# Two norms that follow a finished expert sum: weights spread earlier, the next tile's vector and two turns reordered

## The chip, the cores and the metric

The kernel runs on one core of one Trainium2 chip. The metric is the device time of one execution in microseconds (us). Three executions before the change took 2376.06, 2380.5 and 2389.85 us, median 2380.5. All arithmetic is float32.

## The reference, cut to what matters

Two transformer-like blocks follow each other on 512 rows of 1024 elements. The first ends in a layer of single-neuron experts: each row picks 128 experts (8 heads, 16 each), takes the dot product of its normed vector with 128 rows of `expert_u`, and adds up 128 rows of `expert_v` with the resulting weights. Then it is normed, and the second block begins with a norm of its own.

```python
def one(xb):                      # 64 rows at a time
    ...                           # eidx (rows, 8, 16), gate g
    u = expert_u[eidx]
    v = expert_v[eidx]
    act = jax.nn.gelu(jnp.einsum('td,thkd->thk', xb, u), approximate=False)
    return jnp.einsum('thk,thkd->td', g * act, v)
...
h = h + ff                        # after the experts
out = rmsnorm(h, ln_final)        # end of the first block
# second block
h = rmsnorm_2(x, norm1_g)         # attention and pooling on h @ w_in
x = x + mixed @ w_out
h2 = rmsnorm_2(x, norm2_g)
x = x + (silu(h2 @ w_gate) * (h2 @ w_up)) @ w_down
return rmsnorm_2(x, final_g)
```

## The kernel before, in words

The 512 rows are four tiles of 128. The first block's mixer and expert choice run first, then the second block in the order of `SECOND` (line 38): attention of tiles 0 and 1, attention of tile 2, the feed-forward of tiles 0 to 2, attention of tile 3, its feed-forward, the output.

The experts run beside all this as a second stream. For each tile GpSimd (POOL, L1172) gathers 128 rows of `peer_u`, one indirect DMA of 128 x 4 KB each, into a ring of 16 slots; VectorE (DVE, L2745) takes one dot product per gathered row with the **dot vector**, which stands in two PSUM banks (`wide`, banks 6 and 7): TensorE spreads the norm weights into it (`urow`, L1471) and DVE multiplies it by the tile's row and its factor (L2734). Then 128 rows of `peer_v` are gathered and summed: for tiles 0 and 3 on DVE (L2769), for tiles 1 and 2 (`VPE`) on TensorE in 32 **row units** of four gathered rows each (`rows`, L1481), accumulated in the same banks 6 and 7.

When a tile's sum is complete, the unit `h3` follows. On DVE: the sum is added to the tile (L2776, "h2e"); the tile is multiplied by the norm weights in two halves (L2787, "gained") that TensorE has spread over two banks (`gain`, in the unit `h3` at L1496, eight matmuls); some small operations and a root make the factor (L2791 to L2811); two multiplications write the normed tile (L2815). On ScalarE (ACT): the squares of the tile (L2121), written to banks 6 and 7, the squares of the two halves (L1690), also to banks 6 and 7, and the root (L1678). Banks 6 and 7 are thereby taken by "squares" until ACT is done, and the next tile's `urow` waits for it.

The order of every engine's program is one list of units, made by `make_plan`. The main stream yields after each step; `QUOTA` says how many expert rows are due within each stage of it (in sixths, thirds and so on of the stage's cost), and `more()` appends that much of `plan_experts`. A yield of `("h3", t)` appends all that is left up to tile t's `h3`. Each engine works through its units strictly in the order of the list. PSUM banks are given out by small rings, `lo` (banks 0 to 2) and `hi` (3 to 5) at the places of this change.

Around the end of tile 1 the list reads: row units 28 to 31 between the last steps of choosing tile 3's experts, `h3 1`, one choosing step (L2486), `urow 2`, dots 0 to 3, `chosen`, dots 4 to 6, then `norm` and two `turn` units of the attention of tiles 0 and 1 (a turn transposes a tile on TensorE and scales it by a diagonal matrix that DVE makes at L2244; ACT copies it out at L1734).

Around the end of tile 2 it reads:

```
rows 2 28 | wout 0 1 0 0 | wout 0 1 0 1 | rows 2 29 | norm (fe,0) | turn (fe,0) 0 | rows 2 30
turn (fe,0) 1 | rows 2 31 | h3 2 | norm (at,2) | turn (at,2) 0 | urow 3 | dot 3 0 | dot 3 1
fgate 2 | dot 3 2 | qku 2 0 0 | dot 3 3 | qku 2 0 1 | dot 3 4 | fsoft 2 | dot 3 5 ...
```

`wout` is the attention's output product of tiles 0 and 1 (its result is added at L2667); `norm (fe,0)` and the two turns make the feed-forward's input from it, which is not used before the feed-forward; `turn (at,2)` is tile 2's own, and `fgate`, `qku` and `fsoft` (L2595 on DVE) begin its attention. `IDLE` puts 14 matmuls without use ahead of `turn (at,2)`.

## Time and profile before

| what | value |
|---|---|
| median of three runs | 2380.5 us |
| span of the profiled execution | 2541.9 us |
| its own time apart from the span | not recorded |
| TensorE (PE) busy | 2151.2 us, 85% |
| VectorE (DVE) busy | 1499.3 us, 59% |
| ScalarE (ACT) busy | 653.7 us, 26% |
| GpSimd (POOL) busy | 1020.5 us, 40% |
| moved by DMA | 839.81 MB, mean 330 GB/s |
| mean granted TensorE clock | 0.898 |

The span of the profiled execution is 161.4 us longer than the median of the timed runs, so each time read from the trace belongs to an execution that is slower than the timed ones. A row of the timeline is: start in us from the span's start, duration in us, engine, line, operation, what it writes and reads, count, and in brackets how long the engine was idle before it and what ended that. "remote" stands where no instruction of the trace was found that ended the wait, "issue" where the engine waited for nothing that the profile shows. A float32 matmul has two records.

### The profile page before, as it was taken

How to read it: one execution, taken by the hardware profiler on the slowest of the kernel's cores; microseconds unless marked ns; L12 is line 12 of the kernel's file. 1: busy time of each engine (PE TensorE's matmuls, PEld its weight loads, DVE VectorE, ACT ScalarE, POOL GpSimd, SP SyncE). 2: the span in 40 equal slices, each digit the busy share in tenths (PEclk: the TensorE clock that was granted, in tenths of full speed). 3: DMA queues.
4: the chain of work that ended last, by engine and by line, in shares of the span. 5: the costliest groups of instructions: out<-in, count | busy, mean ns of one | idle time of the engine just before them, and what ended most of it. 6: DMA issues, size and time to landing. Idle time of an engine off the chain costs nothing.

```text
span 2541.9 us, 29123 instructions
## 1 busy us (share of the span) xinstructions
PE 2151.2 (85%) x10694; PEld 1516.7 (60%) x10694; DVE 1499.3 (59%) x3505; ACT 653.7 (26%) x1838; POOL 1020.5 (40%) x1028
## 2 busy tenths in 40 slices
PE   8999998999999986996675366276879799999998
PEld 7999785666666975874431254221366555545695
DVE  3441179999999368647454677710067665886321
ACT  6772235566555121001010101110122000001220
POOL 0000014555665113435566554566544544772000
PEclk8999999999998997998886567578887899999999
DMA  6767568999999978999999888999978998998485
GB/s 237 245 231 240 215 254 298 404 397 393 390 377 337 378 274 320 398 356 380 363 394 361 308 335 320 366 343 364 409 307 323 411 348 313 412 412 355 157 316 173
DMA packets 196750, 839.81 MB, mean 330 GB/s; under 512 B 22000, under 2 KB 22384, under 8 KB 164864
## 3 DMA queue, kind: packets, MB, share of 16 engines
q0 software_dynamic: 147456, 536.94, 54.8%
q1 hardware_dynamic: 43808, 290.72, 30.6%
q10 hardware_dynamic: 5344, 10.29, 1.3%
q8 instruction: 85, 1.39, 0.2%
q14 instruction: 57, 0.47, 0.0%
HBM read 835.70 MB, written 2.16 MB: 330 GB/s over the span
## 4 chain that ended last, share of the span: by engine, by line
PE 60%; DVE 15%; issue 10%; ACT 6%; POOL 5%; another core or an unknown queue 3%; DMA 2%; ACTq 0%; DVEq 0%; SPq 0%
PE ps L1200 59%; DVE rows L2745 7%; POOL rows L1172 5%; DVE ps L2769 1%; DMA rows<-in_pv,eidxT 1%; DVE h L2769 1%; DVE arena L2297 1%; DMA wr<-in_wso 1%; ACT arena L1734 1%; ACT L1871 1%; ACT arena L1865 0%; DMA wr<-in_wgate 0%; ACT L1801 0%; DVE arena L2359 0%
## 5 line engine op out<-in xcount | busy, mean ns | idle before, releaser
L1172 POOL DMA_INDIRECT rows<-in_pu,eidx x512 | 485.3, 948 | 936.6 <-DVE dots L2745 368.7
L1200 PE MATMUL ps<-arena,wr 128*128 128x128 f32 (+4 forms) x3968 | 771.9, 354 | 26.0 <-DMA wr<-in_wso 9.2
L1200 PEld LDWEIGHTS ps<-arena,wr 128*128 128x128 f32 x3968 | 606.9, 195 | 168.6 <-issue 27.3
L2745 DVE CUSTOM_DVE_ANT_0 rows<-rows,ps 128x1024 f32<-128x1024 f32 x512 | 594.0, 1217 | 11.3 <-DMA rows<-in_pu,eidx 5.5
L1200 PE MATMUL ps<-hT,wr 128*128 128x128 f32 (+2 forms) x1600 | 369.7, 390 | 44.6 <-issue 41.3
L1172 POOL DMA_INDIRECT rows<-in_pv,eidx x256 | 289.2, 1130 | 207.0 <-DVE h L2769 101.4
L1200 PEld LDWEIGHTS ps<-hT,wr 128*128 128x128 f32 x1600 | 262.5, 199 | 148.7 <-issue 57.6
L1172 POOL DMA_INDIRECT rows<-in_pv,eidxT x256 | 245.7, 960 | 142.9 <-issue 68.6
L1200 PE MATMUL ps<-rows,wz 128*32 128x512 f32 x1024 | 180.7, 778 | 78.5 <-DMA rows<-in_pv,eidxT 57.1
L1200 PE MATMUL ps<-wr,arena 128*128 128x256 f32 (+2 forms) x704 | 180.7, 412 | 2.1 <-ACT arena L1943 2.1
L2769 DVE SCALAR_TENSOR_TENSOR h<-rows,wgt,h 128x1024 f32<-128x1024 f32 x132 | 169.0, 1280 | 5.7 <-DMA rows<-in_pv,eidx 4.8
L2769 DVE SCALAR_TENSOR_TENSOR ps<-rows,wgt,ps 128x1024 f32<-128x1024 f32 x122 | 156.6, 1284 | 8.1 <-DMA rows<-in_pv,eidx 8.1
L1200 PEld LDWEIGHTS ps<-wr,arena 128*128 128x128 f32 x704 | 129.5, 192 | 49.1 <-issue 33.7
L1200 PEld LDWEIGHTS ps<-rows,wz 128*32 128x32 f32 x1024 | 39.9, 129 | 198.1 <-issue 194.2
L1200 PE MATMUL ps<-wr,fT 128*128 128x512 f32 x304 | 135.2, 602 | 5.5 <-issue 5.5
L1200 PEld LDWEIGHTS ps<-wr,fT 128*128 128x128 f32 x304 | 58.5, 193 | 80.2 <-issue 80.2
L2297 DVE SCALAR_TENSOR_TENSOR arena<-arena,vec 128x144 f32<-128x144 f32 (+2 forms) x160 | 74.8, 468 | 51.9 <-ACT arena L1794 44.7
L2401 DVE TENSOR_TENSOR arena<-arena,ps 128x256 f32<-128x256 f32 (+1 forms) x24 | 12.3, 511 | 151.2 <-PE ps L1200 146.9
L2044 ACT ACTIVATE fT<-ps 128x384 f32<-128x384 f32 (+1 forms) x44 | 16.9, 385 | 276.9 <-PE ps L1200 145.5
L2681 DVE TENSOR_TENSOR fT<-fT,ps 128x384 f32<-128x384 f32 (+1 forms) x44 | 18.5, 421 | 112.7 <-PE ps L1200 86.3
L1200 PE MATMUL ps<-arena 128*128 128x64 f32 (+3 forms) x352 | 64.5, 314 | 11.8 <-DVE arena L2356 6.6
L2633 DVE CUSTOM_DVE_ANT_0 lg<-ps,cb 128x128 f32<-128x128 f32 (+3 forms) x32 | 15.7, 492 | 93.9 <-PE ps L1200 52.2
(403 smaller groups left out, 2258.3 us busy)
## 6 DMA issues: line engine op xcount, KB each, us to landing
wr<-in_wg SPq DMA_DIRECT2D x48, 1024.0 KB
wr<-in_wgu SPq DMA_DIRECT2D x33, 1024.0 KB
wr<-in_wgate SPq DMA_DIRECT2D x24, 1024.0 KB
wr<-in_wso SPq DMA_DIRECT2D x24, 1024.0 KB
wr<-in_wq SPq DMA_DIRECT2D x16, 1152.0 KB
wr<-in_wsc SPq DMA_DIRECT2D x16, 1024.0 KB
wr<-in_wqku SPq DMA_DIRECT2D x15, 1024.0 KB
wr<-in_wdn SPq DMA_DIRECT2D x14, 1024.0 KB
```

The source lines that it names most:

```text
L1172: e.indirect_dma_start(ring[slot_of[i]], None, A[table], bass.IndirectOffsetOnAxis(ap=index[:, t, k:k + 1], axis=0)).then_inc(gathered[slo ...
L1200: return e.matmul(o, l, r, start=start, stop=stop, skip_group_check=True)
L1734: e.activation(dst[:, kk, col:col + w_], b[:, 128 * k:128 * k + w_], ACT.Copy, scale=gv[:, kk:kk + 1]).then_inc(*act.up("turn", tag, s, half))
L1871: e.activation(m[f"mt{c % 2}"].rearrange("p a b -> p (a b)"), fall.rearrange("p a b -> p (a b)"), ACT.Exp, scale=-1.0).then_inc(*act.up("s ...
L2044: e.activation(FD[t0]["fT"][:, j, :], b[:, 0:nr], ACT.Silu).then_inc(*act.up("silu", t0, j))
L2297: e.scalar_tensor_tensor(out=tx[:, c1:n] if k < 3 else xg[:, s_, c1:n], in0=x[:, k + c1:k + n], scalar=W["convw"][:, q4 + k:q4 + k + 1], i ...
L2401: e.tensor_tensor(flat, flat, b[:, 0:2 * nr], MUL).then_inc(*dve.up("mg", q, j))
L2633: e.tensor_tensor_reduce(m[f"lg{p}"][:, 0:kn], b[:, 0:kn], cb[:, h, 0:kn], 1.0, NEG, ADD, ALU.max, mxx[:, p:p + 1]).then_inc(*dve.up("fron ...
L2681: e.tensor_tensor(fT[:, j, :], fT[:, j, :], b[:, 0:nr], MUL).then_inc(*dve.up("fT", t0, j))
L2745: e.tensor_tensor_reduce(row, row, wide[:], 1.0, 0.0, MUL, ADD, dots[:, k:k + 1]).then_inc(*dve.up(*u))
L2769: e.scalar_tensor_tensor(out=sum_, in0=row, scalar=wgt[:, k:k + 1], in1=sum_, op0=MUL, op1=ADD).then_inc(*dve.up(*u))
```

## The change

Five edits, all of order and place:

- `gain` becomes a unit of its own, and for tiles 1 and 2 (those before a tile in `URGENT`) it is put ahead of row unit 28, with its two banks from `hi`. For tiles 0 and 3 it stays behind the sum, in `lo`.
- `h3` is split into the units `h2e`, `gained` and `h3`. For tiles 1 and 2 the next tile's `urow` (TensorE's spread and DVE's multiplication) is put between `gained` and `h3`.
- For tiles 1 and 2 banks 6 and 7 are no longer taken for squares: ACT writes the squares to `junk` (tile 1) or to a tile of the attention that is done (`AT[0]["mx"]`, tile 2), both in SBUF.
- In the attention of tiles 0 and 1, `norm (fe,0)` stays where it was, then `("h3", 2)` is yielded, and the two turns `(fe,0)` come after it.
- The 14 idle matmuls ahead of `turn (at,2)` are taken away.

```diff
@@ -37,6 +37,7 @@
 GROUPS = ((0, 1), (1, 2), (2, 4))
 SECOND = (("attend", 0, 2), ("attend", 2, 3), ("feed", 0, 3), ("attend", 3, 4), ("feed", 3, 4), ("out", 3, 4))
 VPE = (1, 2)
+URGENT = (2, 3)
 VW = 1.5
 SX = 1.8
 PLACES = ("early", "ring", "ring")
@@ -46,7 +47,7 @@
 ARENA = 18144
 AHEAD_GATES = (4, 3, 2)
 GATE_BUFFERS = (4, 3, 2)
-IDLE = {("at", 2): 14, ("at", 3): 2}
+IDLE = {("at", 3): 2}
 AHEAD = 2
 PLAIN = (("at", 3), ("fd", 3),)
 SPARE = 6
@@ -618,7 +619,10 @@
                 wout(hf, part, t)
                 yield True
     if t0 == 0:
-        yield from plan_turn(pl, ("fe", t0), range(nt))
+        fe = plan_turn(pl, ("fe", t0), range(nt))
+        yield from until("normed", fe)
+        yield ("h3", t1)
+        yield from fe
 
 
 def plan_feed(pl, A, t0, t1, outs=()):
@@ -718,10 +722,19 @@
         for half in range(2):
             pl.hold((key, t, half), 6 + half, emptied)
 
+    def gain(t, ring):
+        for half in range(2):
+            pl.take(("gain", t, half), ring, ("dve", "gained" if ("at", t) in PLAIN else "h3", t, half))
+        pl.add("gain", t)
+
+    def urow(t):
+        both("urow", t, ("dve", "dot", t, 127))
+        pl.add("urow", t, v=vc(1024))
+
     for t in range(NT):
         yield ("chosen", t, 0)
-        both("urow", t, ("dve", "dot", t, 127))
-        pl.add("urow", t, v=vc(1024))
+        if t not in URGENT:
+            urow(t)
         for k in range(128):
             if k and k * pieces_of(t) % 128 == 0:
                 yield ("chosen", t, k * pieces_of(t) // 128)
@@ -736,6 +749,8 @@
             yield 1
         both("sums", t, ("dve", "h2e", t))
         for k in range(32):
+            if k == 28 and t + 1 in URGENT:
+                gain(t, "hi")
             if t in VPE:
                 pl.add("rows", t, k)
                 if k < 31:
@@ -745,9 +760,14 @@
                     pl.add("vrow", t, i, v=1.3)
                 if k < 31:
                     yield 4
-        both("squares", t, ("act", "squares", ("h3", t)))
-        for half in range(2):
-            pl.take(("gain", t, half), "lo", ("dve", "gained" if ("at", t) in PLAIN else "h3", t, half))
+        pl.add("h2e", t)
+        if t + 1 in URGENT:
+            pl.add("gained", t)
+            urow(t + 1)
+        else:
+            both("squares", t, ("act", "squares", ("h3", t)))
+            gain(t, "lo")
+            pl.add("gained", t)
         pl.add("h3", t, v=4 * vc(1024))
         yield 4
 
@@ -1493,7 +1513,7 @@
                                    ring[slot_of[i]][:, 512 * half:512 * half + 512], k == 0, k == 31)
                     x.then_inc(*pe.up(*u))
 
-                elif kind == "h3":
+                elif kind == "gain":
                     t = u[1]
                     for half in range(2):
                         b = ps("gain", t, half)
@@ -1683,11 +1703,15 @@
                 w.wait_ge(*dve.at("onemore", *tag))
                 e.activation(l, w_, ACT.Ln).then_inc(*act.up("sp_ln", *tag))
 
+            def squares_of(t):
+
+                return AT[0]["mx"].rearrange("p a b -> p (a b)")[:, 0:1024] if t == 2 else junk if t == 1 else wide
+
             def gained_squares(t):
                 for half in range(2):
                     w.wait_ge(*dve.at("gained", t, half))
                     w.wait_ge(*act.at("first squares", t))
-                    e.activation(wide[:, 512 * half:512 * half + 512],
+                    e.activation(squares_of(t)[:, 512 * half:512 * half + 512],
                                  junk[:, 512 * half:512 * half + 512] if place_of(t)[0] in PLAIN else
                                  bank[pl.bank["gain", t, half][0]][:], ACT.Square, accum_out=se[:, 1 + half:2 + half]
                                  ).then_inc(*act.up("squares", ("h3", t)))
@@ -2112,16 +2136,20 @@
                                          wT[:].rearrange("p (c k) -> p k c", c=4)[:, 4 * z:4 * z + 4, :], ACT.Copy
                                          ).then_inc(*act.up("wz", t, z))
 
-                elif kind == "h3":
+                elif kind == "h2e":
                     t = u[1]
                     ready()
                     if t:
                         w.wait_ge(*dve.at("rsqrt", ("h3", t - 1)))
                     w.wait_ge(*dve.at("h2e", t))
-                    e.activation(wide[:], h2[:, t, :], ACT.Square, accum_out=se[:, 0:1]
+                    if t == 2:
+                        w.wait_ge(*pe.at("wout", 0, 1, 0, 1))
+                    w.wait_ge(*act.last())
+                    e.activation(squares_of(t)[:, 0:1024], h2[:, t, :], ACT.Square, accum_out=se[:, 0:1]
                                  ).then_inc(*act.up("first squares", t))
-                    if place_of(t)[0] not in PLAIN:
-                        gained_squares(t)
+
+                elif kind == "gained" and place_of(u[1])[0] not in PLAIN:
+                    gained_squares(u[1])
 
             for t in range(NT):
                 w.wait_ge(stored[t], 32 if t == NT - 1 else 16)
@@ -2769,7 +2797,7 @@
                         e.scalar_tensor_tensor(out=sum_, in0=row, scalar=wgt[:, k:k + 1], in1=sum_, op0=MUL,
                                                op1=ADD).then_inc(*dve.up(*u))
 
-                elif kind == "h3":
+                elif kind == "h2e":
                     t = u[1]
                     if t in VPE:
                         w.wait_ge(*pe.at("rows", t, 31))
@@ -2777,8 +2805,8 @@
                     else:
                         dve.mark("h2e", t)
 
-
-
+                elif kind == "gained":
+                    t = u[1]
                     plain = place_of(t)[0] in PLAIN
                     for half in range(2):
                         g = bank[pl.bank["gain", t, half][0]]
@@ -2786,6 +2814,10 @@
                         then()
                         e.tensor_tensor(junk[:, 512 * half:512 * half + 512] if plain else g[:], g[:],
                                         h2[:, t, 512 * half:512 * half + 512], MUL).then_inc(*dve.up("gained", t, half))
+
+                elif kind == "h3":
+                    t = u[1]
+                    plain = place_of(t)[0] in PLAIN
                     w.wait_ge(*act.at("first squares", t))
                     then()
                     e.tensor_scalar(se[:, 4:5], se[:, 0:1], 1.0 / 1024, 1e-6, MUL, ADD).then_inc(*dve.up())
```

## Rows read from the trace of the kernel before

**Rows 1.** The page: the span, and the chain that ended last by engine.

```profile
span 2541.9 us, 29123 instructions
...
PE 60%; DVE 15%; issue 10%; ACT 6%; POOL 5%; another core or an unknown queue 3%; DMA 2%; ACTq 0%; DVEq 0%; SPq 0%
```

**Rows 2.** Busy time by stretch: stretch, length, engines, granted clock, DMA share, GB/s.

```profile
1416.00:1440.00 24.00, 6.40 (x36) 5.89 (x32) 10.29 (x19) 4.33 (x9) 8.70 (x10) 0.57 0.68 272
...
1846.00:1866.00 20.00, 13.48 (x102) 12.82 (x100) 8.60 (x20) 5.02 (x15) 4.34 (x5) 0.83 0.48 180
...
2060.00:2335.00 275.00, 268.75 (x746) 141.30 (x747) 196.88 (x199) 13.39 (x23) 149.73 (x135) 0.99 0.93 366
```

**Rows 3.** Timeline around the end of tile 1's sum, 1395 to 1470.

```profile
1412.46 3.64 PE L1200 MATMUL ps<-rows,wz 128*32 128x512 f32 x16 [3.77 <-DMA rows<-in_pv,eidxT]
...
1416.03 2.59 PE L1200 MATMUL ps<-con,vec 128*128 128x128 f32 x16
1416.39 1.22 DVE L2776 TENSOR_TENSOR h<-h,ps 128x1024 f32<-128x1024 f32 x1 [10.93 <-PE ps L1200]
...
1423.46 0.70 DVE L2787 TENSOR_TENSOR ps<-ps,h 128x512 f32<-128x512 f32 x1 [5.84 <-remote]
...
1430.49 0.70 DVE L2787 TENSOR_TENSOR ps<-ps,h 128x512 f32<-128x512 f32 x1 [6.33 <-remote]
...
1431.96 3.79 PE L1200 MATMUL ps<-con,vec 128*128 128x128 f32 x16 [13.35 <-ACT ps L1690]
...
1437.66 1.28 DVE L2734 SCALAR_TENSOR_TENSOR ps<-h,rs,ps 128x1024 f32<-128x1024 f32 x1
```

**Rows 4.** Timeline ahead of the end of tile 2's sum, 1825 to 1846.

```profile
1827.57 1.92 PE L1200 MATMUL ps<-rows,wz 128*32 128x512 f32 x16
...
1831.31 0.69 DVE L2667 TENSOR_TENSOR h<-h,ps 128x512 f32<-128x512 f32 x1 [5.61 <-remote]
...
1835.23 3.78 PE L1200 MATMUL ps<-junk,h 128*128 128x128 f32 x16 [5.74 <-DVE junk L2244]
...
1838.94 2.64 PE L1200 MATMUL ps<-rows,wz 128*32 128x512 f32 x16
...
1841.51 2.05 PE L1200 MATMUL ps<-junk,h 128*128 128x128 f32 x16
...
1843.49 1.92 PE L1200 MATMUL ps<-rows,wz 128*32 128x512 f32 x16
```

**Rows 5.** Timeline behind the end of tile 2's sum, 1845 to 1871.

```profile
1845.35 2.05 PE L1200 MATMUL ps<-con,vec 128*128 128x128 f32 x16
...
1846.14 1.22 DVE L2776 TENSOR_TENSOR h<-h,ps 128x1024 f32<-128x1024 f32 x1 [10.90 <-PE ps L1200]
...
1850.39 0.70 DVE L2787 TENSOR_TENSOR ps<-ps,h 128x512 f32<-128x512 f32 x1 [3.02 <-remote]
...
1853.27 0.70 DVE L2787 TENSOR_TENSOR ps<-ps,h 128x512 f32<-128x512 f32 x1 [2.18 <-remote]
...
1854.73 0.35 DVE L2797 SCALAR_TENSOR_TENSOR se<-se 128x1 f32<-128x1 f32 x2 [0.31 <-ACT ps L1690]
...
1856.80 1.41 DVE L2815 TENSOR_SCALAR h<-ps,se 128x512 f32<-128x512 f32 x2
...
1857.69 3.56 PE L1200 MATMUL ps<-xf,h 128*128 128x128 f32 x16 [5.49 <-DVE h L2815]
1859.86 1.14 ACT L1734 ACTIVATE hT<-ps,vec 128x128 f32<-128x128 f32 x4 [4.54 <-PE ps L1200]
...
1861.09 1.95 PE L1200 MATMUL ps<-con,vec 128*128 128x128 f32 x16
...
1863.15 1.29 DVE L2734 SCALAR_TENSOR_TENSOR ps<-h,rs,ps 128x1024 f32<-128x1024 f32 x1 [4.95 <-PE ps L1200]
...
1870.30 0.16 DVE L2595 TENSOR_TENSOR xx<-ps,vec 128x8 f32<-128x8 f32 x1
```

**Rows 6.** Timeline of TensorE in the row units of tile 2, 1783 to 1791.

```profile
1786.85 0.59 PE L1200 MATMUL ps<-rows,wz 128*32 128x512 f32 x1 [0.82 <-issue]
```

## The prediction, made before the changed kernel ran

> **What bounds the kernel now.** I read the page first. The chain that ended last lies 60% on TensorE (PE) and 15% on VectorE (DVE), and 3% of it is time that ended with no releaser in the trace [rows 1]. No engine bounds the whole, so the change has to be read where it sits. The busy time by stretch shows two holes: in the 24 us behind tile 1's sum DVE is busy 10.3 us and the DMA share is 0.68, and in the 20 us behind tile 2's sum 8.6 us and 0.48. From 2060 to 2335 PE is busy 268.8 of 275 us [rows 2]. So what is gained at tile 2's sum moves the start of tile 2's attention and of the feed-forward, which PE then carries to the end at its own pace. Tile 3's experts run beside that and end in time: what only they gain is worth nothing.
>
> Last I read the timeline of both places. Behind tile 1's sum (row unit 31 ends at 1416.1) come, all on DVE, the sum's addition, the two gained halves, the factor, the normed tile and the dot vector at 1437.7 [rows 3]. The gained halves waited 5.84 and 6.33 us with no releaser. The eight matmuls that they need had run from 1416.03 to 1418.62. Ahead of tile 2's sum PE does row unit 29, stands 5.74 us for the diagonal of the turns (fe,0), then does turn, row unit 30, turn, row unit 31, one after the other up to 1845.4 [rows 4]. Behind it the same DVE series follows, the turn (at,2), and only behind this turn the dot vector's matmuls, for which DVE stands 4.95 us [rows 5].
>
> **Which of these waits are in the timed runs.** The span is 2541.9 us, the median 2380.5: 161.4 us of the profiled execution are not in the timed ones. In the trace PE at times issues one matmul per 1.41 us (0.59 busy, 0.82 idle for nothing that shows) in the middle of row units whose others take 0.12 us each (1.92 for 16) [rows 6, 4]. Such stalls, and semaphores that seem to arrive late, are what I take the 161 us to consist of. I therefore work out the sum without the waits that have no releaser (5.84 + 6.33 at tile 1; 5.61 ahead of tile 2's sum, and 3.02 + 2.18 behind it) [rows 3 to 5], and keep a case in which they are real. The Trainium skill, in NOTIFIC — the notification-queue block, section 3 (Interfaces), says that this block presses back on the producers of records when an internal FIFO fills, and that this can stall an engine. By that rule the stalls belong to the recording; no row here shows it, and the sum without it would be that of the second case below.
>
> **Tile 2, ahead of the sum.** Let 0 be the end of the last output product, 1827.6. Before: DVE's addition 0.69, then ACT's squares, root and DVE's diagonals. From the end of that addition (1832.00) to the turn that waited for them (1835.23) are 3.2 us, so the diagonals are there at 4.0. Then turn 3.78, row unit 2.64, turn 2.05, row unit 1.92 as recorded [rows 4], end at 14.4; with the first turn and unit at the pace of the second ones, 2.05 and 1.92, it is 11.9. After: the spreading of the norm weights, moved ahead of row unit 28, costs PE 2.05 on the same path [rows 5], as PE works without a gap there, so all starts at 2.05. Units 29, 30 and 31 need 3 x 1.92, end 7.8; DVE gets through the diagonals at 6.1 and waits for the sum. The sum is complete 4.1 to 6.6 us earlier. Had the gathered rows landed? Units 30 and 31 ran at 1838.9 and 1843.5 with no wait for a DMA; whether the rows were there 8 us earlier is not shown. I take it so, as unit 29 ran straight behind the output product; if they were only just in time, this part is worth nothing (case 3).
>
> **Tile 2, behind the sum.** 0 is now the start of the addition. Before: 1.22, gained halves 0.70 each, the second not ahead of the spreading's end (2.05), so 2.8; squares of the second half 0.7, 3.5; from L2797 (1854.73) to the end of the normed tile (1858.21) 3.5, so 7.0, its first half at 6.3. The turn (at,2) then takes 2.05 to 3.56, the dot vector's matmuls 1.95, its multiplication 1.28: first dot at 11.6 to 13.1 [rows 5]. After: 1.22 + 1.40 = 2.6. The dot vector's matmuls start when the addition is done, at 1.3, and take 1.95 at full clock or 3.79 at half clock [rows 5, 3], so DVE waits for them 0.6 to 2.5 us. Its multiplication ends at 4.6 to 6.4, the two small operations ahead of L2797 take it to 4.9 to 6.7, the rest 3.5: the normed tile is done at 8.4 to 10.2, which is 1.4 to 3.2 later than before, and the first dot starts there, 2.9 to 3.2 earlier. ACT's squares are hidden under the dot vector's multiplication.
>
> What comes next is late for another reason. The two turns (fe,0) are yielded after tile 2's sum and are 3.4 of some 31 us of planned cost of their stage (`wout`), two thirds of its last sixth, for which `QUOTA` has 7 expert rows due: this puts 4 to 5 dots of tile 3 between the sum and the attention that had stood behind it. L2595, where the attention's gates enter DVE, had 5 dots ahead of it (1864.5 to 1870.3 at 1.14 each [rows 5]) and will have 9 or 10. Before: 11.6 to 13.1 plus 5.7, so 17.3 to 18.8. After: 8.4 to 10.2 plus 11.4, so 19.8 to 21.6, that is 2.5 to 2.8 later. By ACT: four halves of turns (fe,0), 1.14 each [rows 5], start behind the root and push the copies of turn (at,2), and with them PE's `fgate`, back by 2 to 2.5 us. Either way the stretch behind the sum loses about 2.5 and the stretch ahead of it gains 4.1 to 6.6: a gain of 1.6 to 4.1. I take 3, the middle, since half of the row that is longest (3.78) belongs to a PE that had stood 5.74 us.
>
> The turns had stood between row units that were ready, so their 4.1 to 5.8 us on PE are no cost in the new place: PE stood idle there for the normed tile (5.49 [rows 5]). The 14 idle matmuls gave nothing but the clock. In the stretch of tile 2 the granted clock averages 0.83, in that of tile 1 0.57 [rows 2], between the levels 2.4 and 1.2 GHz. The turns now stand where the idle matmuls were. The Trainium skill, in TensorE: Matmul & The Clock Gate, Part 1, says that the throttled state is the default and that activity releases it; by it, real turns do the idle matmuls' work, but a turn that waits for ACT's copies does not. A turn (at,2) at half instead of full clock would cost 1.5 us by the rows (3.56 against 2.05), which is within my bounds.
>
> **Tile 1.** Its row units wait for gathers (3.77 ahead of unit 31 [rows 3]), so spreading the norm weights ahead of unit 28 costs nothing; without that cover it would be 2.6. Before, without the unreleased waits: 1.22, gained halves until 3.3 (the spreading took 2.59), squares 4.0, to the normed tile 7.5, the choosing step between 2.3, dot vector 1.3: first dot at 11.1. After: 2.6; the dot vector's matmuls end at 5.1 (half clock, 3.79) or 3.3 (full); normed tile 10.2 or 8.4; choosing step: first dot at 12.5 or 10.7. That is 1.4 later or 0.4 earlier; the clock there is near half, so +0.5. The wait for the norm weights has only been exchanged for one for the dot vector's matmuls, as no time is left between the sum and its use.
>
> **Squares to SBUF.** ACT's squares of a tile change the place of their output; bounded by nothing below and 0.1 us above from the nearest rows (1.14 for four copies to SBUF is 0.28 each [rows 5]), under other work. Zero.
>
> **Sum.** -3 at tile 2, +0.5 at tile 1: 2.5 us less. Against the profiled execution that would be 2539.4; its other waits I carry as the second case. For the median: 2378.
>
> **The rivals.**
> 1. Likeliest, 2378, own range 2373 to 2382: the sum above.
> 2. The waits without a releaser are in the timed runs too, and the change removes them. Tile 2: 5.2 (gained halves) and 4.95 with 1.29 for the dot vector come on top, and the half-clock turn, so about 12 us at L2595 instead of 3. Tile 1: up to 12.2 less the same kind of wait for the dot vector's matmuls, say 5. Together 12 to 20: 2360 to 2368. For it: they lie on the chain [rows 1, 3, 5]. Against it: the 161 us, and that a late semaphore would hold up the new wait as the old.
> 3. Nothing is moved: something else sets the end, gathers (DMA share 0.68 and more outside the holes) or the weights of the attention. 2380 to 2381. For it: PE's plan of tile 1 changes by nothing, and a stream that is fed earlier fills its 16 slots and stands.
> 4. Slower. DVE works in order, and the dot vector now stands ahead of the factor: the normed tile, the turns and the whole attention wait for PE's eight matmuls. If these come as late as the gained halves' did (5.84 to 6.33), each tile loses about 5 us, and the 5 extra dots add 5.7 at tile 2: up to 12 us more than case 1's gains, 2386 to 2393. It decides once the delay of these matmuls is over 4 us at both tiles while the old waits were shorter.
>
> **Chances.** Case 1 0.48, case 2 0.26, case 3 0.16, case 4 0.10. A measurement of this kernel can tell about 0.5% (11.9 us) from no change: the three runs shown lie 13.8 us apart. Faster by more needs under 2368.6: case 2, 0.25. Slower by more needs over 2392.4: half of case 4 and a measure of chance, 0.07. The rest, 0.68, is within. The range, from case 2's fast end to the low part of case 4, is 2360 to 2387.
>
> **What the profile after would show.** Right: between row unit 29 and tile 2's addition no turn and no wait for L2244; the addition 8 to 11 us earlier behind the last output product; L2734 ahead of L2791 at tiles 1 and 2, waiting 0.6 to 2.5 us for PE; turns (fe,0) between the sum and turn (at,2); 9 or 10 dots ahead of L2595. Wrong: L2787's waits stay although the norm weights are spread long before (then they are no semaphore of `gain`), or L2734 waits over 4 us (case 4), or the time from tile 2's addition to L2595 shrinks by over 5 us (case 2), or PE has new waits for gathers at row units 30 and 31 (case 3). The prediction fails if stalls of recording and stalls of the kernel can't be parted as I did.

## The result and the profile after

The changed kernel takes 2401.3 us (median of 6 runs, 2393.73 to 2407.48) against 2381.38 (6 runs, 2376.06 to 2389.85): 1.0074 of the time before, 95% interval 1.0054 to 1.0094. It is slower by 0.74%, some 18 us, where the forecast had 2378 us and a range that ended at 2387. Two executions in later sets, 2829.0 us of the kernel before and 8738.16 us of turns_only, ran at a granted clock of 0.72 and 0.22 and are left out of the medians and ratios.

The profile of rows 1 to 6 is 161 us longer than the median of the timed runs. So the kernel before was profiled twice more, unchanged: `b_again` (span 2382.0 us) and `b_third` (span 2385.3). In neither is one of the waits without a releaser of [rows 3 to 5]: the 161 us belonged to that one recording, as the sum had assumed. Below, "before" is one of these two. The changed kernel's profile belongs to the fastest of its six runs (2393.73 us), 7.6 us under their median, so part of the timed loss is not in it. First its page.

```profile
span 2391.9 us, 29066 instructions
```

The timeline at the end of tile 2's sum, the changed kernel, which answers to [rows 4, 5].

```profile
1718.26 5.64 PE L1220 MATMUL ps<-rows,wz 128*32 128x512 f32 x48
...
1723.96 1.22 DVE L2804 TENSOR_TENSOR h<-h,ps 128x1024 f32<-128x1024 f32 x1 [1.77 <-PE ps L1220]
...
1725.23 2.05 PE L1220 MATMUL ps<-con,vec 128*128 128x128 f32 x16 [1.33 <-DVE h L2804]
...
1727.32 1.29 DVE L2762 SCALAR_TENSOR_TENSOR ps<-h,rs,ps 128x1024 f32<-128x1024 f32 x1 [0.68 <-PE ps L1220]
...
1732.65 1.21 DVE L2773 CUSTOM_DVE_ANT_0 rows<-rows,ps 128x1024 f32<-128x1024 f32 x1
...
1738.52 2.23 ACT L1758 ACTIVATE hT<-ps,vec 128x128 f32<-128x128 f32 x8 [4.56 <-issue]
...
1740.89 3.56 PE L1220 MATMUL ps<-wsm,hT 128*128 128x8 f32 x16 [6.64 <-ACT hT L1758]
...
1744.48 0.17 DVE L2623 TENSOR_TENSOR xx<-ps,vec 128x8 f32<-128x8 f32 x1
...
1751.35 0.17 DVE L2200 TENSOR_SCALAR sq<-sq 128x8 f32<-128x8 f32 x1 [5.88 <-ACT sq L1702]
```

The same places in the kernel before (`b_third`).

```profile
1732.18 1.22 DVE L2776 TENSOR_TENSOR h<-h,ps 128x1024 f32<-128x1024 f32 x1 [7.67 <-PE ps L1200]
...
1742.70 1.85 PE L1200 MATMUL ps<-wsm,hT 128*128 128x8 f32 x16
1742.98 1.29 DVE L2734 SCALAR_TENSOR_TENSOR ps<-h,rs,ps 128x1024 f32<-128x1024 f32 x1 [3.42 <-PE ps L1200]
...
1744.41 1.22 DVE L2745 CUSTOM_DVE_ANT_0 rows<-rows,ps 128x1024 f32<-128x1024 f32 x1
...
1750.12 0.16 DVE L2595 TENSOR_TENSOR xx<-ps,vec 128x8 f32<-128x8 f32 x1
...
1751.17 0.17 DVE L2172 TENSOR_SCALAR sq<-sq 128x8 f32<-128x8 f32 x1 [0.27 <-ACT sq L1682]
```

Read them side by side. Row units 29 to 31 now run as one block, and the sum's addition comes 8.2 us earlier (4.2 of it are there at tile 1's addition already, 1365.3 against 1369.5, so 4.0 belong to the stretch between the two sums). The attention's gates enter DVE (L2595, now L2623) 5.6 us earlier. One instruction later, at the exponential's result (L2172, now L2200), it is 0.2 us later than before: DVE stands 5.88 us for ScalarE (ACT). The whole gain is gone 27 us behind the sum, before the attention's heads begin.

The loss comes 300 us on. The timeline at the feed-forward's last gate product (fT 21) and first down product, the changed kernel, then before (`b_third`).

```profile
2052.52 0.56 DVE L2709 TENSOR_TENSOR fT<-fT,ps 128x384 f32<-128x384 f32 x1 [4.98 <-PE ps L1220]
2052.99 1.28 DVE L2797 SCALAR_TENSOR_TENSOR h<-rows,wgt,h 128x1024 f32<-128x1024 f32 x1
...
2066.12 1.28 DVE L2797 SCALAR_TENSOR_TENSOR ps<-rows,wgt,ps 128x1024 f32<-128x1024 f32 x1
2067.31 0.55 DVE L2709 TENSOR_TENSOR fT<-fT,ps 128x384 f32<-128x384 f32 x1
...
2067.97 5.37 PE L1220 MATMUL ps<-wr,fT 128*128 128x512 f32 x8 [5.24 <-issue]
```

```profile
2052.18 0.55 DVE L2681 TENSOR_TENSOR fT<-fT,ps 128x384 f32<-128x384 f32 x1 [4.98 <-PE ps L1200]
2052.65 1.28 DVE L2769 SCALAR_TENSOR_TENSOR h<-rows,wgt,h 128x1024 f32<-128x1024 f32 x1
...
2061.01 1.28 DVE L2769 SCALAR_TENSOR_TENSOR ps<-rows,wgt,ps 128x1024 f32<-128x1024 f32 x1
2062.50 0.55 DVE L2681 TENSOR_TENSOR fT<-fT,ps 128x384 f32<-128x384 f32 x1 [0.21 <-PE ps L1200]
...
2063.16 10.11 PE L1200 MATMUL ps<-wr,fT 128*128 128x512 f32 x23 [0.76 <-issue]
```

Tile 3's sum is made on DVE, one addition for each gathered row (L2797, before L2769); the expectations below call these additions row units. Between the last two gate products stand 12 of them, where 8 stood. They follow each other every 1.19 us, so the last product is 14.8 instead of 10.3 us behind the one before it. TensorE (PE) had finished its inputs at 2062.7 and stands 5.24 us, not 0.76, and behind the stall it works at half clock for a while. The busy time by stretch (columns as in [rows 2]) from 2068 to 2080 shows this: the changed kernel, a second profile of it (`a_again`, span 2395.1), and before.

```profile
2068.00:2080.00 12.00, 12.00 (x24) 5.19 (x25) 12.00 (x11) 0.00 (x0) 9.56 (x9) 0.86 1.01 400
```

```profile
2068.00:2080.00 12.00, 9.15 (x17) 4.13 (x18) 12.00 (x11) 0.00 (x0) 9.87 (x8) 0.72 1.02 410
```

```profile
2068.00:2080.00 12.00, 12.00 (x30) 5.30 (x29) 12.00 (x11) 0.00 (x0) 9.87 (x8) 1.00 1.02 413
```

A granted clock of 0.86 over 12 us is 1.7 us of full-speed work lost, 0.72 is 3.4 us. Tile 3's own sum is none the later: its gained halves start at 2174.3 in the changed kernel, at 2178.0 before. But PE reaches the turn that needs it at 2184.8 instead of 2178.3, and from there to the end everything is 6.5 us later.

### The profile page after: what moved, and what is told of

Read it like the earlier page. It is cut to its first block and busy times, and to the rows that moved or that the text cites. A ratio compares the mean times of both kernels' runs of the same rounds, so it can differ in the third digit from the quotient of the medians.

```text
span 2391.9 us, 29066 instructions
## 1 busy us (share of the span) xinstructions
PE 2091.1 (87%) x10666; PEld 1486.1 (62%) x10666; DVE 1500.3 (63%) x3505; ACT 652.1 (27%) x1838; POOL 1019.9 (43%) x1028
## 5 line engine op out<-in xcount | busy, mean ns | idle before, releaser
L1220 PE MATMUL ps<-arena,wr 128*128 128x128 f32 (+4 forms) x3968 | 767.3, 353 | 11.8 <-DMA wr<-in_wso 9.3
L1220 PE MATMUL ps<-hT,wr 128*128 128x128 f32 (+2 forms) x1600 | 352.3, 382 | 17.7 <-DVE xx L2623 15.7
L1220 PEld LDWEIGHTS ps<-hT,wr 128*128 128x128 f32 x1600 | 255.6, 195 | 111.1 <-issue 16.9
L1220 PE MATMUL ps<-rows,wz 128*32 128x512 f32 x1024 | 161.8, 764 | 93.7 <-DMA rows<-in_pv,eidxT 92.4
L2797 DVE SCALAR_TENSOR_TENSOR h<-rows,wgt,h 128x1024 f32<-128x1024 f32 x132 | 169.1, 1281 | 3.3 <-DMA rows<-in_pv,eidx 2.4
L2797 DVE SCALAR_TENSOR_TENSOR ps<-rows,wgt,ps 128x1024 f32<-128x1024 f32 x122 | 156.7, 1285 | 10.2 <-DMA rows<-in_pv,eidx 10.2
L2068 ACT ACTIVATE fT<-ps 128x384 f32<-128x384 f32 (+1 forms) x44 | 16.9, 385 | 251.5 <-PE ps L1220 190.8
L2695 DVE TENSOR_TENSOR h<-h,ps 128x512 f32<-128x512 f32 x8 | 5.5, 688 | 104.3 <-PE ps L1220 104.3
```

Source lines behind the costliest of these rows:

```text
L1220: return e.matmul(o, l, r, start=start, stop=stop, skip_group_check=True)
L2068: e.activation(FD[t0]["fT"][:, j, :], b[:, 0:nr], ACT.Silu).then_inc(*act.up("silu", t0, j))
L2695: e.tensor_tensor(hv, hv, b[:], ADD).then_inc(*dve.up("wout", t0, hf, t))
L2797: e.scalar_tensor_tensor(out=sum_, in0=row, scalar=wgt[:, k:k + 1], in1=sum_, op0=MUL, op1=ADD).then_inc(*dve.up(*u))
```

## The experiments

Ratios are to the kernel before, run on the same chip in turn. "Heads" are tile 2's attention heads, "five dots" the dot products of tile 3 that the moved turns draw ahead of tile 2's attention. The medians of different runs were taken on different chips, so a ratio compares two of them better than their medians do.

**b_again: the kernel before, again.**

> The kernel before, unchanged, profiled once more. If the long waits without a releaser (5.84 and 6.33 us at tile 1's sum, 5.61 and 5.2 at tile 2's) belong to one recording, this span is near 2380 us and they are gone: the first half of tile 1's gained product follows the sum's addition within 1 us. If they belong to the kernel, the span is again near 2540 us.

2383.84 us. The waits of 5.6 to 6.3 us are gone; tile 1's gained halves (L2787) follow the addition at once. This settles the forecast's second case.

**vec_only: all but the turns' move.** The turns (fe,0) in their old place, with the 14 idle matmuls.

```diff
-        fe = plan_turn(pl, ("fe", t0), range(nt))
-        yield from until("normed", fe)
-        yield ("h3", t1)
-        yield from fe
+        yield from plan_turn(pl, ("fe", t0), range(nt))
...
-IDLE = {("at", 3): 2}
+IDLE = {("at", 2): 14, ("at", 3): 2}
```

> Norm weights ahead of row unit 28, the next tile's dot vector ahead of the norm and the squares to SBUF; the turns (fe,0) stay between the row units and the 14 idle matmuls stay. Theory A (the loss comes from the turns' new place): within 4 us of the kernel before, ratio 0.998 to 1.002. Theory B (the loss comes from DVE's wait for the dot vector ahead of the factor): slower, 1.005 or more.

2393.93 us, 1.0052 (1.0035 to 1.0070). By the number this is theory B's forecast and not A's, but B's mechanism is not in the rows: DVE stands 0.68 us for the dot vector's matmuls at both tiles, as in the changed kernel. See vec_one to vec_again.

**turns_only: the turns' move alone**, with the idle matmuls left out, in the kernel before (the reverse edit).

> The turns (fe,0) behind tile 2's sum and no idle matmuls, all else as before. Theory A: 1.005 or more, the whole loss of about 18 us. Theory B: 0.998 to 1.001, as the sum of tile 2 is complete 4 to 6 us earlier and the attention behind it 2 to 5 us later.

2406.23 us, 1.0096 (1.0073 to 1.0118), as theory A had it and B had not. PE stands 5.2 us ahead of the first down product here too.

**no_dots: the whole change, without the five dots.** The turns' planned cost is charged before the sum is called for and taken back after, so the turns stand where the change puts them but draw nothing.

```diff
         yield from until("normed", fe)
+        pl.p += nt * mmc(128)
+        yield True
         yield ("h3", t1)
-        yield from fe
+        for _ in fe:
+            pass
+        pl.p -= nt * mmc(128)
```

> The whole change, but the five dots of tile 3 that the moved turns drew ahead of tile 2's attention stand behind its start again, as before. In the profile after, ScalarE's copies of tile 2's turn start at 1738.5, 4.3 us after the turn's matmuls, when VectorE is through the fifth of these dots. Theory A1 (these dots are the loss): ratio to before 1.000 to 1.003, and the copies start within 0.5 us of the matmuls. Theory B: 1.006 or more, as the changed kernel.

2384.48 us, 1.0005 (0.9987 to 1.0023): with the five dots back behind the attention's start the whole loss is gone. The sum is as early as in the changed kernel and nothing is gained by it. At the exponential DVE stands even longer, since ACT runs in order and two copies of the q product stand ahead (timeline of `no_dots`):

```profile
1741.69 0.17 DVE L2627 TENSOR_TENSOR xx<-ps,vec 128x8 f32<-128x8 f32 x1 [0.68 <-PE ps L1224]
...
1745.30 0.28 ACT L1998 ACTIVATE qT<-ps 128x128 f32<-128x128 f32 x1 [6.81 <-PE ps L1224]
1747.53 0.28 ACT L1998 ACTIVATE qT<-ps 128x128 f32<-128x128 f32 x1 [1.95 <-PE ps L1224]
1747.82 1.28 ACT L1706 ACT_TABLE_LOAD   x1
1749.12 0.21 ACT L1706 ACTIVATE sq<-sq 128x8 f32<-128x8 f32 x1
1749.36 0.17 DVE L2204 TENSOR_SCALAR sq<-sq 128x8 f32<-128x8 f32 x1 [6.73 <-ACT sq L1706]
```

**a_heads, b_heads, a_idle: is it the clock?** In the profiles of the changed kernel, vec_only and no_dots PE fell to half clock in the heads; in b_again it did not. So I formed a rival: the change loses clock there. The edit of the first two (a_idle puts `("at", 2): 14` back into `IDLE`):

```diff
                     b = ps(*u)
+                    if t == 2:
+                        for _ in range(4):
+                            mm(b[:, 0:128], ident, ident, True, True)
```

> The changed kernel with four idle matmuls of 128x128 ahead of each of the eight score products of tile 2's heads (32 in all, 1.8 us at full clock). In the profiled executions of the changed kernel and of the three earlier partial versions the granted clock was at its lower level (0.50) for about 20 us of these heads, and in the second profile of the kernel before it was not; the same heads lasted 30.2 us and 23.0 us. Theory C (what the change loses is clock: TensorE falls to 1.2 GHz in tile 2's heads): the clock of the heads stays above 0.9, the heads last 24 to 25 us, and the time comes down by 5 to 7 us, to some 2394 to 2396 us by the median of 2401.3. Theory A1 (the five dot products of tile 3 ahead of tile 2's attention are the loss, the heads' clock falls in the kernel before just as often): no gain, 2400 to 2403 us; or, if the clock does stay up, kernel before and after both gain alike.

> The kernel before with the same 32 idle matmuls in tile 2's heads. Theory C (the clock falls there because of the change): nothing to give back, ratio to the kernel before 1.000 to 1.001. Theory A1 (the fall belongs to both kernels): the same gain as in the changed kernel with them, whatever it is; if the matmuls hold the clock up, 3 to 7 us faster than the kernel before, 2375 to 2379 us.

> The changed kernel with the 14 idle matmuls ahead of tile 2's turn put back (128x128, the one other thing that the change takes away with the turns' move). Between 1720 and 1780 us the granted clock of the changed kernel's profile lost 7 us more than in the kernel before. Theory C (clock): the clock of 1720 to 1780 comes back to some 0.95 and the time falls by 2 to 4 us, to 2397 to 2399 us. Theory A1 (five dots, and ScalarE held until they are done): TensorE waits there for copies that wait for the dots, so a warmer clock gives nothing back: 2400 to 2403 us.

a_heads 2396.2 us, 1.0053 (1.0036 to 1.0071); b_heads 2383.44, 1.0002 (0.9988 to 1.0016); a_idle 2396.67, 1.0064 (1.0046 to 1.0082). By the numbers both runs of the heads are what theory C had forecast. The matmuls do hold the clock up, but about a quarter of the loss is all that comes back, and the interval of a_heads overlaps the changed kernel's. The 5.2 us stall stands in both changed versions. The matmuls also cost more than the 1.8 us of the expectation: with them the heads, from the first score product to the last value product, last 25.5 us, against 28.7 in the changed kernel at a clock of 0.65, and 21.3 in b_again, which has none and kept its clock (0.98).

**b_third: does the kernel before fall too?**

> The kernel before, unchanged, for a third profile. Theory C expects tile 2's heads at full clock (mean 0.9 and more, some 23 us) as in the second profile; Theory A1 expects that they fall to 0.50 in some executions of this kernel too, so that here they may last 28 to 31 us; the time stays within 2372 to 2390 us.

2387.11 us, and it falls, so the fall belongs to both kernels. Two other runs, with one profile each, say that it is not the main cause: the heads of no_dots fell too (0.67) and its time is that of the kernel before, and those of b_quota, below, kept the clock (0.98) and it lost 0.6%. Busy time by stretch in the heads, first b_again, then b_third, the changed kernel, a_heads.

```profile
1790.00:1812.00 22.00, 18.87 (x106) 13.61 (x107) 19.22 (x53) 9.81 (x25) 8.44 (x9) 0.94 1.02 409
```

```profile
1790.00:1812.00 22.00, 20.78 (x85) 15.52 (x83) 15.56 (x43) 7.87 (x22) 7.49 (x8) 0.63 0.89 339
```

```profile
1790.00:1812.00 22.00, 20.77 (x80) 15.40 (x81) 14.86 (x42) 7.70 (x21) 6.58 (x8) 0.61 0.87 340
```

```profile
1790.00:1812.00 22.00, 22.00 (x132) 15.91 (x131) 12.75 (x41) 7.63 (x18) 6.57 (x7) 1.00 1.01 403
```

From the gates' entry on DVE to the end of the heads it is 57.4 us in b_again, 64.0 in b_third and 70.7 in the changed kernel. The first difference, 6.6 us, is the clock, which the same program has in one execution and not in another. The second, 6.7, is mostly DVE's wait for the exponential (5.88 instead of 0.27).

**a_quota, b_quota: five units by one number.** `QUOTA` says how many units of tile 3 are due in each part of a stage. One of its numbers takes the five back, or gives them to the kernel before, from the first third of tile 2's attention stage on. a_quota, in the changed kernel:

```diff
-('attend', 2): (12, 7, 4)
+('attend', 2): (7, 7, 4)
```

b_quota, in the kernel before: 12 becomes 17.

> The changed kernel with one number of the hand-written quotas lowered by five: 12 to 7 for the first third of tile 2's attention stage. The five dot products of tile 3 still stand ahead of that attention, but from the middle of it on every dot product and row unit of tile 3 stands where it stood before the change. In the changed kernel they stand five further ahead, and so twelve row units of tile 3's sum, not eight, stand on VectorE ahead of the feed-forward's last gate product (fT 21); TensorE stood still for 5.24 us there against 0.76. Theory O (the change loses by what the five do to the order behind them): the stall is gone (0.8 to 1.3 us), the end of the attention of tile 2 stays where the changed kernel has it, and the time falls by 5 to 9 us to 2392 to 2396 us. Rival A1 (the five cost at the attention's own start, where ScalarE is held): the time stays within 2 us of 2401.3.

> The kernel before with the same quota raised from 12 to 17: nothing of the change, but tile 3's stream drawn five units further ahead from tile 2's attention on, so that twelve row units stand ahead of the last gate product as in the changed kernel. Theory O: a stall of 4 to 6 us of TensorE ahead of the first down product, and 2387 to 2391 us against 2382 (ratio 1.002 to 1.004). Rival A1: no stall and no loss from this order alone, 2381 to 2385 us; a loss over 9 us would say that the dot products inside the attention cost as well.

a_quota 2389.96 us, 1.0040 (1.0025 to 1.0055); b_quota 2395.68 us, 1.0060 (1.0037 to 1.0084). The kernel before becomes slow by that number alone, more than I had expected, and the stall is there (timeline of b_quota; 12 row additions between the two gate products):

```profile
2050.39 0.55 DVE L2681 TENSOR_TENSOR fT<-fT,ps 128x384 f32<-128x384 f32 x1 [4.98 <-PE ps L1200]
...
2065.19 0.54 DVE L2681 TENSOR_TENSOR fT<-fT,ps 128x384 f32<-128x384 f32 x1
...
2065.84 7.50 PE L1200 MATMUL ps<-wr,fT 128*128 128x512 f32 x10 [5.23 <-issue]
```

Taken away from the changed kernel it is gone, and the first product follows as before (timeline of a_quota):

```profile
2063.38 0.55 DVE L2709 TENSOR_TENSOR fT<-fT,ps 128x384 f32<-128x384 f32 x1 [0.21 <-PE ps L1220]
2064.03 9.25 PE L1220 MATMUL ps<-wr,fT 128*128 128x512 f32 x21 [0.76 <-issue]
```

From a gate product near the end (fT 20) to the end of the program it is 339.4 us in the changed kernel, 339.7 in a_again, 340.6 in b_quota; 333.5, 333.1 and 332.4 in b_again, b_third and a_quota. The order costs 6 to 8 us in the profiles. It is so in every recording but the first one: the six with 12 additions take 339.4 to 340.6 us for this part, the thirteen with 8 take 332.4 to 335.0.

But the number does not move the far place alone. Ahead of tile 2's first score product stand 24 dots before and in a_quota, 29 in b_quota and in the changed kernel. So the five cost a second time, on DVE inside the attention's start. The spans, from the start of tile 2's addition to fT 20 and from there to the end, in us:

| recording | sum to fT 20 | fT 20 to end | clock of the heads |
|---|---|---|---|
| b_again | 313.6 | 333.5 | 0.98 |
| b_quota | 318.3 | 340.6 | 0.98 |
| b_third | 320.0 | 333.1 | 0.67 |
| no_dots | 324.1 | 332.6 | 0.67 |
| a_quota | 325.2 | 332.4 | 0.65 |
| after | 328.6 | 339.4 | 0.65 |
| a_again | 328.8 | 339.7 | 0.66 |
| turns_only | 332.9 | 339.5 | 0.66 |

Against b_again, at the same clock, b_quota loses 4.7 us in the first part and 7.1 in the second, 11.8 of its 12.8 timed. The expectation's own sign, a loss over 9 us, says the same: the dots inside the attention cost as well. From the changed kernel to a_quota it is 3.4 and 7.0 us, 10.4 where the medians differ by 11.3 and the ratios by 8; to no_dots it is 4.5 and 6.8.

**soft_first: the gate ahead of the q and k products.** In no_dots, `fsoft` of tile 2 is put ahead of the first two products, so that ACT's exponential no longer stands behind their copies.

```diff
+    if t0 == 2:
+        pl.add("fsoft", t0, v=2.0)
+        yield True
     for s3 in range(4):
...
-        if s3 == 0:
+        if s3 == 0 and t0 != 2:
```

> The kernel of the run no_dots (the whole change, the five dot products behind the attention's start as before) with the forget gate's soft function ahead of tile 2's first two q and k products in the order, where it stood behind them. In no_dots VectorE stood 6.73 us for ScalarE's exponential, which was queued behind ScalarE's copies of those products; in the kernel before this was 0.27 us, since there the gate's product came late. Theory O adds: this wait is where the earlier sum was given back; with the order turned it falls under 2 us, VectorE is 4 to 6 us earlier at the heads and the time is 2 to 5 us below no_dots, 2379 to 2382 us. Rival (weights, gathers or the clock set the attention's pace): the wait goes but the heads start no earlier than 1785 to 1788 us, and the time is that of no_dots within 1.5 us.

2384.84 us, 1.0004 (0.9988 to 1.0019). The 6.73 us wait is gone and the time does not move: that wait alone is not the lever. In this profile the heads ran at 0.50 from 1796 to 1808, and from the sum to fT 20 it is 320.7 us, 3.3 less than in no_dots; but PE stood 3.39 us for gathered rows ahead of row unit 31, which it did not in no_dots, and so the sum came that much later.

**a_again: the changed kernel, second profile.**

> The changed kernel once more, for a second profile and one more time: 2393 to 2407 us. Theory O expects the stall of TensorE ahead of the first down product again (4.5 to 8 us) and 12 row units ahead of the last gate product. The clock's rival expects the granted clock of tile 2's heads to be the larger difference from the kernel before, of which the three profiles show it at full level in one, and at 0.50 in two.

2396.98 us. The stall is there (5.23 us), 12 row additions ahead of the last gate product, and the heads ran at 0.57 from 1796 to 1812. One row ahead of tile 2's sum differs from the first profile:

```profile
1724.59 1.92 PE L1220 MATMUL ps<-rows,wz 128*32 128x512 f32 x16 [3.03 <-DMA rows<-in_pv,eidxT]
```

Row unit 31 waits for its gathered rows. It does so for 3.0 to 3.4 us in four of the nine recordings of the changed kernel and its variants (a_again, soft_first, nd_heads, soft_heads) and not in the other five. In b_again and b_third, whose turns stand between the row units, it does not wait.

**vec_one, vec_two, vec_none, vec_again: what vec_only lost.** `URGENT` picks the tiles: `(2,)` is tile 1's sum alone, `(3,)` tile 2's alone, `()` neither.

> The first three edits at tile 1's sum alone (norm weights spread ahead of row unit 28, the dot vector of tile 2 ahead of the norm); tile 2's sum, the turns and the idle matmuls as before. The forecast held tile 1's edit to cost 0.5 us: 2382 to 2384 us against 2382.5. Theory T1 (vec_only's 11 us sit at tile 1, where the normed tile and with it the next tile's projections of the two-tile query come 1.3 us later and TensorE's clock falls): 2389 to 2394 us, ratio 1.003 to 1.005. Theory T2 (they sit at tile 2): ratio 1.000 to 1.001.

> The same edits at tile 2's sum alone. The forecast held them, without the turns' move, to gain 1 to 3 us: 2379 to 2382 us. Theory T2 (vec_only's loss sits here: VectorE goes earlier into the dot products, ScalarE and TensorE come later, VectorE stands 4.3 us for the gate's exponential, and the attention's TensorE work falls to 1.2 GHz in more executions): 2389 to 2394 us. Theory T1: 2380 to 2384 us.

> Neither tile's early spread nor early dot vector: what is left of the edits is the place of the squares (in SBUF for tiles 1 and 2) and the first squares' split from the rest. The forecast held this to be free: 2381 to 2384 us, ratio within 0.9990 to 1.0010. If it is 2389 us or more, vec_only's loss is the squares' and not the vector's, against both T1 and T2.

> The kernel of vec_only once more, for a second profile: 2388 to 2397 us. If it is above 2393 us, the row by row difference from the first profile (2388.43 us) shows where the typical execution loses its 5 us more; the theories say in the granted clock of TensorE between tile 1's sum and the end of tile 2's heads (its half-clock time there larger by 5 to 15 us), and not in the feed-forward or at tile 3's sum.

vec_one 2382.41 us, 1.0001 (0.9984 to 1.0018); vec_two 2390.34, 1.0029 (1.0011 to 1.0046); vec_none 2384.4, 1.0006 (0.9989 to 1.0023). Tile 1's edit and the squares' place are free as far as this can tell. The early dot vector at tile 2 is not a gain without the turns' move, but a small loss against the kernel before, as theory T2 had the number; its interval overlaps that of vec_none. vec_again took 2382.51 us, outside its expectation and below all six runs of vec_only (2388.43 to 2396.86). Its heads ran at a clock of 1.00, those of vec_two at 0.67. From the gates' entry to the end of the heads they take 62.6 and 69.7 us, their spans are 2380.7 and 2389.6. Both have the 5.9 us wait for the exponential, which eats what the earlier dots give.

**nd_heads, soft_heads: both places of the lost gain.** no_dots and soft_first with the 32 matmuls of a_heads.

> The kernel of no_dots (1.0005 of the kernel before; heads at a granted clock of 0.50 for 20 us in its profile) with four idle matmuls of 128x128 ahead of each of the eight score products of tile 2's heads, as in a_heads and b_heads. They held the clock at 1.00 in a_heads and took the changed kernel from 2401.3 to 2396.2 us; in the kernel before they changed nothing (1.0002). Theory H (the early sum's gain is lost in the heads' clock): clock of the heads at 0.95 or more, 2377 to 2380 us, ratio 0.997 to 0.999. Rival E (it is lost earlier, to VectorE's wait of 6.7 us for ScalarE's exponential, and what the clock gives back the 32 matmuls cost): 2382 to 2385 us, ratio 0.9995 to 1.001.

> The kernel of soft_first (1.0004 of the kernel before) with the same 32 idle matmuls: both places of loss are taken away at once. Theory H and E together: 2374 to 2378 us, ratio 0.996 to 0.998. If it too is at 2382 to 2385 us, neither place held the gain, and the attention's pace is set by something else that no earlier sum can move.

nd_heads 2384.52 us, 1.0003 (0.9993 to 1.0014); soft_heads 2379.99 us, 0.9984 (0.9969 to 1.0000). Held in this way, the clock alone gives nothing; as the matmuls leave the heads at 25.5 us and not at 21, this doesn't say what a clock kept for nothing would give. Only with wait and clock both treated is there a hint of the early sum's gain, 3 us, and its interval ends at no change. It is the fastest version of the study. PE waited 3.3 us for gathered rows at row unit 31 in both profiles.

## Why the prediction was wrong

**What bounds the kernel now.** This is the step that failed. It said that tile 3's experts "run beside that and end in time: what only they gain is worth nothing". They do end in time. But DVE works through the experts' units and the feed-forward's gate products in one order. Five units drawn ahead at about 1735 shift the whole order by five until 2067, where a group of four row additions slips in front of the product that the first down product waits for. I counted the five, put them on DVE at tile 2's attention, and did not follow them to where PE is busy throughout. The price there is 4.5 us of stall and 1.7 to 3.4 us of half clock, 6 to 8 us by the profiles. The timed differences are larger, 13 us by the medians for b_quota and 11 between the changed kernel and a_quota, because the same number also moves five dots at the attention's start (4.7 and 3.4 us in the table).

**Tile 2, ahead of the sum.** The sum's mechanism was right where the rows had landed. From the last output product to tile 2's addition it is 11.5 us before (11.9 was forecast), 5.6 after, and the spreading costs 2 us ahead of it: 3.9 us gained, where 4.1 to 6.6 was forecast. In a_again it is 8.6, and 1.0 us is gained: row unit 31 stands 3.03 us for its gathered rows. That is the doubt of case 3, which so came true in part, in four of nine recordings. From tile 1's addition to tile 2's it is 365.4 and 362.7 us before, 358.7 and 361.5 after, 4 us on the mean. The sign "8 to 11 us earlier behind the last output product" did not come (5.9 and 2.9) and did not follow from the forecast's own sum, which gives 6.1 to 8.6.

**Tile 2, behind the sum.** DVE's part came out within the forecast: first dot 8.7 us behind the addition (8.4 to 10.2), gates' entry 20.5 (19.8 to 21.6) against 17.9 before (17.3 to 18.8), DVE's wait for the dot vector's matmuls 0.68 (0.6 to 2.5). The gates' 20.5 is in part luck. In a_quota only 8 dots stand ahead of them, not 10, and they enter 20.5 us behind the addition all the same, since DVE stands for PE's `fgate`:

```profile
1748.34 0.17 DVE L2623 TENSOR_TENSOR xx<-ps,vec 128x8 f32<-128x8 f32 x1 [2.40 <-PE ps L1220]
```

Two paths that end together, DVE's dots and ACT's copies with `fgate` behind them, gave the number that the forecast had worked out from the dots alone. The 5.49 us of idle PE that were to take the turns (fe,0) are 1.83 in b_again and b_third; turn (at,2) starts 8.3 us behind the addition where it started 6.9 behind it. ACT's part was mis-sized: `fgate` was to come 2 to 2.5 us later relative to the sum and comes 6.4 later (16.9 instead of 10.5). ACT's copies of turn (at,2) first wait for the marker of the attention's start on DVE, and the five dots stand ahead of this marker: the 4.56 us of ACT's row at 1738.52. In no_dots, without the five, it is 1.8 later. And one wait was missed: the exponential on ACT behind the q copies. So of a net gain of 3 us nothing reached the heads. The stretch from the sum to fT 20 was to lose 2.5 us and loses 8.6 (b_third against after, at the same clock); 4.5 of them go when the five dots go (no_dots). By timing, no_dots is 5.5 us below a_quota by the medians (8 by the ratios). The profiles of the two show 1.1 us of it in this stretch and nothing behind it; the rest is not pinned to a row.

**Tile 1.** +0.5 was forecast. The first dot comes 10.9 and 11.1 us behind the addition in the two profiles of the changed kernel, 11.0 and 11.2 before, and vec_one is at 1.0001. Free, as forecast to within what can be told.

**Squares to SBUF.** Zero was right: vec_none 1.0006 (0.9989 to 1.0023).

**The idle matmuls.** Nothing speaks against "gave nothing but the clock": with them put back, a_idle is at 1.0064 (1.0046 to 1.0082) beside the changed kernel's 1.0074 (1.0054 to 1.0094), no difference that the runs can show.

**The rivals.** Case 2 (the waits without a releaser are real) falls by b_again. Case 3's reason, gathered rows that are only just in time, is seen at row unit 31 in some executions. Case 4 had the right sign by the wrong mechanism: the wait for the dot vector is 0.68 us, not over 4, and its "5 extra dots add 5.7 at tile 2" is the part that was true: 4.7 us in b_quota. Its range of 2386 to 2393 still ends below the measured 2401.

**What stays open.** vec_only was 1.0052 in one set of runs, and its parts are at 1.0001, 1.0006 and 1.0029. Its profile is no help: from the sum on it takes 320.5 and 333.1 us, as b_third does. The profiles of the changed kernel show some 15 us more than b_third behind the sum (8.6 to 8.8 and 6.3 to 6.6), less what the sum gains ahead of it, against a timed loss of 18 to 20. Their runs are 4 and 8 us faster than the changed kernel's median, and that of b_third is 4 us slower than the median of the kernel before. The heads' clock differs from execution to execution and is worth 7 us. Without added matmuls it fell in 12 of the 15 recordings behind the first: in all seven with the turns moved, in five of the other eight. Whether the changed kernel loses it more often than the kernel before is neither shown nor excluded. It could be part of vec_only too: the mean clock of the whole execution is under 0.930 in five of its six runs, and in four of the 16 of the kernel before on that chip. Over all sets, the 39 executions of the kernel before with a mean clock of 0.934 or more average 2379.0 us, the 17 with 0.927 or less 2386.7.

## What to carry to other kernels

When a move changes how much interleaved work is drawn ahead, count the shift through to the end of that stream, and look at every later place where one of its units stands in front of something that a full engine waits for; hand-set quotas hold for one order only. A gain ahead of a junction counts only up to the next wait of another engine, so follow all engines past it, with each marker and each queue entry ahead. And test such a shift alone in the old kernel: one changed number showed here in one run what the diff had hidden, once it was also counted what else that number moved. Set the profiled execution beside the spread of the timed ones, too: here it was the fastest of six, and it showed less of the loss than the timing did.

## What the runs showed of the hardware

TensorE can fall to half clock while it is busy. In the heads of b_third it was busy 20.78 of 22 us and the granted clock averaged 0.63; its only gap there was 1.22 us, ahead of the first short matmuls of 128x64. Two stretches of it:

```profile
1790.00:1796.00 6.00, 4.78 (x28) 3.21 (x26) 5.43 (x15) 2.71 (x8) 1.87 (x2) 0.98 1.00 407
1796.00:1802.00 6.00, 6.00 (x19) 3.98 (x18) 3.60 (x12) 2.17 (x6) 2.42 (x3) 0.50 1.02 406
```

The same program kept 0.94 in b_again, where it was busy 18.87 of the 22 us. With 4 matmuls of 128x128 added per head the clock of the heads was 1.00 in all four versions that have them. It isn't free: the heads last 25.5 us with them, 21 at full clock without, 28 to 29 at half clock without. The Trainium skill, in TensorE: Matmul & The Clock Gate, Part 1, says that activity releases a clock that is throttled by default; the rows agree in that added matmuls kept it up. They do not agree with a reading by idle gaps alone, since the engine was busy nearly throughout.

What is transferred does not follow the clock at once: the two stretches above moved 407 GB/s at 0.98 and 406 at 0.50. Over 1790 to 1812 b_again moved 409 GB/s and b_third 339, but vec_none moved 404 at a clock of 0.74 and nd_heads 345 at 1.00. And one recording (mean clock 0.898) can be 161 us longer than the median of the timed runs, with waits of 5 to 6 us that two other recordings of the same program don't have.
